# Holding back the first transfers, five dummy products fewer, and 2 MB of weights ahead of a store, in a two-layer mixture-of-experts trunk

## What is computed

```
for layer in (0, 1):
    if layer == 0:                       # mixer A: gated chunks; mixer B: sparse attention
        xn = rms_norm(x, mix_norm_even)
        proj = xn @ w_in                 # 512 x 1024 by 1024 x 2328
        au, av, q, kc, vc, ks, vs, kw, vw, gl = split(proj)
        x = x + concat(gating(au, av), attention(q, kc, ..., gl)) @ w_out
    else:                                # mixer C: windowed means of 2, 4, 8, 16 rows
        x = x + pool(rms_norm(x, mix_norm_odd))
    xn = rms_norm(x, ffn_norm[layer])
    # top 1 of 4 expert groups, then top 2 of its 8 experts, 32 experts in all
    x = x + sum over the chosen experts e of
            weight * ((silu(xn @ w_gate[e]) * (xn @ w_up[e])) @ w_down[e])
```

## Time and profile before

| | us |
|---|---|
| median of 3 executions | 809.83 (809.79 to 810.35) |
| the profiled execution, whole | 810.39 |
| its span, first to last instruction | 808.6 |
| TensorE busy in the span | 760.3 (94%) |
| VectorE busy | 259.3 (32%) |
| ScalarE busy | 251.2 (31%) |
| GpSimd busy | 104.0 (13%) |
| bytes moved | 258.69 MB, mean 320 GB/s |

### The profile page before, as it was taken

The page is one execution under the profiler, slowest core; times in us unless marked ns, Lnnn a source line. Parts: engine busy times, 40 slices in busy tenths (PEclk is TensorE's granted clock), DMA queues, the critical chain, the costliest instruction groups (busy, mean ns, idle before and its releaser), DMA issues.

```text
span 808.6 us, 9731 instructions
## 1 busy us (share of the span) xinstructions
PE 760.3 (94%) x3822; PEld 356.3 (44%) x3824; DVE 259.3 (32%) x654; ACT 251.2 (31%) x599; POOL 104.0 (13%) x170
## 2 busy tenths in 40 slices
PE   8999999999999999999988989979999999977987
PEld 7544544555555654333333333369333333332322
DVE  1011517675646365111110011376631111111015
ACT  4421346464444632121121112256222112111112
POOL 3000000000000001212422112250111121101111
PEclk9999999999999999999998989999999999999999
DMA  8995225132010679999999999999999999999998
GB/s 336 347 342 226 94 77 209 53 131 105 1 40 1 214 295 344 423 423 426 420 426 427 425 421 420 401 431 408 401 409 426 424 424 424 427 425 426 422 403 322
DMA packets 39703, 258.69 MB, mean 320 GB/s; under 512 B 8145, under 2 KB 8529, under 8 KB 26600
## 3 DMA queue, kind: packets, MB, share of 16 engines
q1 hardware_dynamic: 31016, 242.22, 74.0%
q0 software_dynamic: 8640, 15.83, 5.2%
HBM read 247.46 MB, written 26.21 MB: 338 GB/s over the span
## 4 chain that ended last, share of the span: by engine, by line
PE 85%; DMA 5%; DVE 4%; issue 4%; ACT 2%; SPq 0%; POOL 0%; POOLq 0%; DVEq 0%
PE ps L2202 28%; PE ps L2220 13%; PE ps L1893 12%; PE ps L2044 7%; PE ps L2196 4%; PE ps L1960 3%; PE ps L2102 3%; PE ps L1972 2%; PE ps L2111 2%; DMA norm<-expert_rows 2%; DMA expert_rows<-tmp 2%; PE ps L2149 2%; PE ps L1875 2%; PE ps L2209 1%; DVE x_rows L1308 1%
## 5 line engine op out<-in xcount | busy, mean ns | idle before, releaser
L2202 PE MATMUL ps<-w_pair,tmp 128*64 128x512 f32 x704 | 165.1, 620 | 17.3 <-issue 14.6
L2202 PEld LDWEIGHTS ps<-w_pair,tmp 128*64 128x64 f32 x704 | 52.8, 142 | 112.0 <-issue 105.9
L1893 PE MATMUL ps<-w_pair,norm 128*128 128x512 f32 (+1 forms) x256 | 98.6, 545 | 1.2 <-DMA w_pair<-in_w_in_chunk_dram 1.2
L1282 DVE TENSOR_TENSOR tmp<-tmp,ps 128x256 f32<-128x256 f32 x32 | 13.5, 421 | 249.0 <-ACT tmp L1141 249.0
L1141 ACT ACTIVATE tmp<-ps 128x256 f32<-128x256 f32 x32 | 12.3, 384 | 231.1 <-PE ps L2202 231.1
L2202 PE MATMUL ps<-norm,tmp 128*64 128x512 f32 x320 | 74.0, 617 | 6.0 <-issue 6.0
L2220 PE MATMUL ps<-w_pair,tmp 128*64 128x512 f32 x296 | 70.1, 599 | 1.1 <-ACT tmp L1144 0.9
L1893 PEld LDWEIGHTS ps<-w_pair,norm 128*128 128x128 f32 x256 | 48.2, 190 | 48.7 <-issue 44.4
L828 POOL DMA_INDIRECT expert_rows<-tmp x30 | 30.2, 1005 | 304.5 <-DVE tmp L1740 278.4
L822 POOL DMA_INDIRECT tmp<-norm_rows,tmp x30 | 31.1, 1035 | 262.1 <-DVE tmp L1660 237.7
L1740 DVE COPY tmp<-ps 128x512 f32<-128x512 f32 x30 | 20.8, 692 | 89.1 <-PE ps L2220 89.1
(11 more groups left out here) (288 smaller groups left out, 879.2 us busy)
## 6 DMA issues: line engine op xcount, KB each, us to landing
w_pair<-in_gate_up_by_row_dram SPq DMA_DIRECT2D x30, 2048.0 KB, 27.6
norm<-in_gate_up_by_row_dram SPq DMA_DIRECT2D x18, 2048.0 KB, 20.5
w_pair<-in_down_by_pair_dram SPq DMA_DIRECT2D x15, 2048.0 KB, 33.0
w_pair<-in_gate_up_by_row_dram SPq DMA_DIRECT2D x28, 1024.0 KB, 10.8
rest<-in_down_by_pair_dram SPq DMA_DIRECT2D x10, 2048.0 KB, 27.9
w_pair<-in_w_in_chunk_dram SPq DMA_DIRECT2D x4, 2048.0 KB, 14.6
norm<-expert_rows SPq DMA_DIRECT2D x16, 512.0 KB, 7.1
expert_rows<-tmp SPq DMA_DIRECT2D x1, 4096.0 KB, 41.6
```

The lines of the kernel that those rows point to most:

```text
L1282: return ve.tensor_tensor(out, in0, in1, op)
L1893: ins = mm(bank(4 + i % 4)[:, 0:n], xT[:, b, k, :], w[:, k, :], start=(k == 0), stop=(k == KD - 1))
L2202: ins = mm(o[64 * a:64 * a + 64, :], xT[:, k, 64 * a:64 * a + 64], gu[w][:, a, 2 * FE * k:2 * FE * (k + 1)], start=(k == 0), stop=(k == KD ...
```

## The change

Three places are edited. SyncE waits for block 0's columns and the gains (`s_gain`, 32) before it issues block 1's columns and everything behind them. Five of the ten dummy products with the identity are left out. In layer 1, expert 1's 2 MB of pair 2 are issued ahead of the store of block 3 and of the 0.5 MB of pair 4, instead of behind them.

```
             load_win(0, slice(0, 4))
             load_win(0, slice(4, KD))
+            sp.wait_ge(s_gain, 32)
             sp.dma_start(columns[1], t["x_by_column"][1]).then_inc(s_xc1, 16)
...
                     load_down_extra(1, back)
+                    load_gate_up(1, 2, 1)
                     store_rows(NB - 1)
                     load_down_early(1, 1)
-                    load_gate_up(1, 2, 1)
                     sp.wait_ge(s_st, 16 * NB * 2)
...
             pe_.wait_ge(s_const, 2)
-            for _ in range(10):
+            for _ in range(5):
                 mm(bank(7)[:, 0:P], ident[:, :], ident[:, :], start=True, stop=True)
```

## The result

| | before | after |
|---|---|---|
| median of 20 executions each, us | 809.89 (808.29 to 811.63) | 811.90 (810.56 to 813.60) |
| ratio, 95% interval | | 1.0024 (1.0018 to 1.0030) |
| profiled execution, whole / span, us | 810.39 / 808.6 | 810.56 / 808.8 |

The changed kernel is 2.0 us slower. The predicted 811.2 and its range hold the time, but the border of 811.4 for "slower by over 0.2%" is passed, and I had given that side 0.27. The profiled execution of the changed kernel is the fastest of its 20, so the two spans differ by 0.2 us only. A difference of two spans is therefore no measure here; the traces are read for what happens in them, and times are taken from medians and ratios.

What follows compares the result with a forecast made beforehand. The first chunk's transfer was taken to bound the start, the DMA engines layer 1. Terms 0 + 1.2 + 0.2 = 1.4 us more gave 811.2 median (811.8 profiled), range 807.9 to 812.8.

Steps and rivals of the forecast that it cites:

- Part 1: Start: SyncE's wait delays later issues 1.7 us, covered by chunk 0's transfer; cost 0, gain at most 2.6 us.
- Rival 1: Start: SyncE's issues disturb the chunk; held back, it lands at 6.2 to 7.5, giving 808.2; chance 0.28 with the filled hole.
- Part 2: Start: five dummies fewer widen TensorE's gap to 2.6 us and the clock falls; cost 1.2 us, bounds 0 and 1.4.
- 10 x 0.143 = 1.4 us: Start: ten of 20 dummy records, which take 2.86 us, are saved, so TensorE's dummies end at 6.0 instead of 7.43.
- on the far side of the gap that fell: Start: a 2.6 us gap lowers the clock, since it fell behind 1.93 us and not behind 1.41; a fall costs 1.7 us.
- what the first real product gains or loses goes through to the end of the first stage: First stage: the chain has no transfer behind the first product, so its shift of one or two us persists.
- Part 3: Layer 1, about 562 to 580 us: 2 MB ahead of the last store; 0.2 us lost, bounds 0 and 2.1.
- The queue is just long enough: Layer 1, store landing at 577.3: 0.5 MB, 1.2 us, still queued covers the restart, or runs dry for a moment.
- about a us: Layer 1, SyncE's release by the store: time a fresh issue needs to show in the transfer rate.
- Rival 3: Layer 1, 577 us: the DMA queue runs dry, 2.1 us; 813.1 with the clock's 1.2, 811.9 without; chance 0.10.
- the other hole (564 to 568): Layer 1: low rates of 315 and 209 GB/s; if the earlier 2 MB filled it, 1.6 us would come back.
- The gather: Layer 1: GpSimd's gather of pair 1's rows waits for the store; a us late delays TensorE under one, covered by later waits.

Runs made afterwards that it cites:

- hold: Only SyncE's wait for x's first columns and the gain added to the kernel before: 810.01 us against 810.17, ratio 1.0001.
- d5: Only five of the ten identity dummy products left out of the kernel before: 809.94 us against 810.17, ratio 1.0002.
- swap: Only layer 1's 2 MB of pair 2 moved ahead of the last store, against the kernel before: 811.06 us against 810.17, ratio 1.0014.
- hold_d5: The wait and five dummies fewer, without the 2 MB move, against the kernel before: 811.19 us against 809.95, ratio 1.0013 (0.9998 to 1.0028).
- after_fed: Whole change plus 1 MB of pair 4's down weights issued ahead of SyncE's store wait, against the kernel before: 810.30 us against 809.95, ratio 1.0009.
- d0: No identity dummy products, against the kernel before with ten: 811.35 us against 809.89, ratio 1.0020.
- d30: Thirty identity dummy products instead of ten, against the kernel before: 813.34 us against 809.89, ratio 1.0046.
- swap_fed: The 2 MB move plus 1 MB of pair 4's down weights ahead of SyncE's store wait, against the kernel before: 810.40 us against 809.89, ratio 1.0006.
- hold_swap: The wait and the 2 MB move, all ten dummies kept, against the kernel before: 811.89 us against 810.17, ratio 1.0022.
- swap_last: The 2 MB and also pair 4's 0.5 MB ahead of the store, against the kernel before: 812.47 us against 809.89, ratio 1.0029.

## Why the prediction was right and wrong

**Part 1, cost 0: right.** The second columns were issued at 4.41 (said: 4.3) and landed at 10.96, no later than before. TensorE's second block waited 0.34 us for their scaling in the changed kernel's trace, as they landed 3.0 us behind the chunk there, against 2.7 in the kernel before and in hold; in hold's trace the second block follows the first without such a wait, and hold alone is at +0.1 us. The reading of the slow rate as start-up and not as crowding holds as well: from 4 to 6 us the traces without the wait have 186 to 345 GB/s (d5 323, swap 327), those with it 228 to 327 (the changed kernel 244). The rate of these two us varies from execution to execution, and it is no sign of a crowd. Rival 1 falls with it: the chunk never landed ahead of 7.5.

**Part 2, cost 1.2: wrong for the changed kernel.** Two of its signs failed: the gap was 1.44 us and not 2.3 to 2.6, and no slow stretch came behind it. The first step that failed is "10 x 0.143 = 1.4 us", by which the dummies were to end at 6.0. The 20 records of the earlier trace rows do not have one pace, since the clock's first record in that trace is at 5.5 us, in the midst of them; five dummy products took 2.02 us in the changed kernel, 1.98 in hold_d5, 2.34 in after_fed and 1.43 in d5, where that record is at 4.9. Together with a chunk that landed at 7.98 instead of 8.56 this took 1.2 us off the gap. That d5 had a gap of 2.19 and hold_d5 one of 1.61 is the dummies alone: the chunk landed at 8.13 and 8.11.

The second is the rule that a gap is "on the far side of the gap that fell". The clock did fall behind the 2.19 us of d5, and the second block's products start at 13.74 there (the text said near 14). But a gap's length alone does not decide. In the trace that I had read, the clock stood at 1.00 behind a gap of 2.17 us at 527.96 and went to 0.50 behind those of 1.93 and 2.39 us; in the changed kernel's it stayed at 1.00 behind 2.38 us at 748.55 and went to 0.50 behind 1.54 us at 473.35. The Trainium skill (TensorE: Matmul & The Clock Gate, section Why this matters for your kernels) asks for no idle gap over about 3 us; these traces have the fall behind 1.54, 1.93, 2.19 and 2.39 us.

The third is "what the first real product gains or loses goes through to the end of the first stage", taken as the cost of the whole kernel. The shift of d5's trace is 1.5 us at layer 0's experts, 0.9 us in bytes at 760, and 0.2 us in the median of its executions, with 1.1 as the upper bound. d0 and d30, with larger shifts, arrive with 1.6 and 3.7. How much of a fall's 1.4 us would arrive stays open.

**Part 3, cost 0.2: wrong, and this was the result.** The orders came as described: the 2 MB landed at 574.9 (said: 576), the store at 576.1 (577.3), and SyncE issued the next load at 576.16. The step that failed is "Before, 2.5 MB or 6 us of transfers were queued at that moment; now only the 0.5 MB, 1.2 us ... The queue is just long enough". It has two faults. The first: it treats sixteen DMA engines as one that ends everything at one time. A transfer is spread over sixteen, and its landing is that of the slowest. By the semaphore events of the trace the sixteen ends of the store lie between 572.94 and 576.14 in the changed kernel, and between 570.18 and 572.44 before. Their ends of the 0.5 MB behind it begin at 574.1, and nine of sixteen had ended by 576.0: more than half of the engines had nothing left when SyncE was released at 576.1. So the rate falls from 574 on, 2 us ahead of the landing, which is what the windows show. The move does not make the spread: over the fourteen traces it lies between 2.3 and 3.9 us. The 6 us queued before cover it, 1.2 us don't. The Trainium skill (DMA: Bandwidth & Descriptors, section Why a DMA increments its semaphore by 16 and not by 1) says it: a transfer runs on up to sixteen engines which finish independently, and only the full count means that it has landed. The trace agrees, with 3.2 us between the first and the last. I knew the count and did not put it into the sum.

The second fault: the "about a us" until a fresh issue shows in the rate was taken as all that has to be covered. The windows of the changed kernel behind the issue at 576.16:

```profile
576.00:577.00 1.00, 1.00 (x4) 0.20 (x4) 0.93 (x3) 0.78 (x4) 0.01 (x1) 1.00 0.25 102
577.00:578.00 1.00, 1.00 (x8) 0.29 (x4) 0.90 (x6) 0.98 (x3) 1.00 (x1) 1.00 1.39 262
578.00:579.00 1.00, 1.00 (x8) 0.49 (x4) 0.90 (x7) 0.96 (x2) 0.06 (x1) 1.00 0.60 229
579.00:580.00 1.00, 1.00 (x7) 0.41 (x7) 1.00 (x3) 0.70 (x3) 0.00 (x0) 1.00 1.01 426
```

The full rate is back nearly 3 us behind the issue. My text had this slow start in its upper bound, from the rows at 154 us, and left it out of the 0.2. No run separates the two. An estimate from the changed kernel's trace: against the kernel before, some 1.0 MB or 2.4 us of the full rate are missing from 574 to 580; the store's sixteen ends are at 574.8 in the mean and SyncE is released at 576.1, so the spread has 1.3 us of it, and the restart the other 1.1.

Rival 3 had mechanism, place and price: 2.1 us and 811.9 without the clock, a window from 578 to 580 with a DMA share below 0.8 (it was 0.80, and 0.67 from 574 to 576). It came in at 1.6 us for the move alone and 811.90 for the whole. Its chance of 0.10 was too low for what its own price and rows said. The doubt about the other hole (564 to 568) told nothing: over all traces its rate goes from 262 to 418 GB/s, with and without the move.

**The gather: right.** It was released by the store and TensorE waited 0.63 us for it, and by swap_fed 1.71 us of such a wait went with +0.5 us at the end, while hold_swap had no such wait and +1.8.

**The sum.** 811.2 came from 1.2 in part 2 and 0.2 in part 3; by the runs of the parts it should have been about 0.2 and 1.6. That the time fell into the range, and near the forecast, is luck: two errors of opposite sign, with the loss forecast in another place than where it arose.

## What to carry to other kernels

Before you move a transfer ahead of one that is waited for, add up what is still queued behind the latter on each DMA engine, and ask that it covers the spread between the first and the last engine's end plus the restart until the full rate is back, not only the mean; when it doesn't, put an independent load between the store and the wait. Where a later stage runs at the full rate of the DMA engines, bytes that are not moved in a hole are the price of it, in us at that rate. What a delay of TensorE ahead of it costs is not known from its size: here a small one was lost in the noise and two larger ones arrived. And when two traces differ by less than the spread between executions, compare what is in them (bytes moved by a given time) and not their spans.

## What the runs showed of the hardware

- The sixteen DMA engines' ends of one transfer of 0.5 MB were 2.3 us apart before and 3.2 us in the changed kernel, and between 2.3 and 3.9 us over all fourteen traces.
- A queue of transfers that has run dry takes some us to be at the full rate again: in the changed kernel 426 GB/s were back at 579, nearly 3 us behind the issue at 576.16; in swap_last nothing moved from 578.0 to 578.5 behind the issue at 577.70, and the rate was 328 GB/s at 581.
- The start of the program has a spread of its own: the chunk's first half (0.6 MB) landed between 7.7 and 8.6 us, and 186 to 345 GB/s were moved from 4 to 6 us, whatever SyncE issued behind it.
- TensorE's clock went to its level of 1.2 GHz behind gaps of 1.54, 1.93, 2.19 and 2.39 us and stayed at 2.4 GHz behind gaps of 1.44, 2.17 and 2.38 us. One and the same wait, that ahead of pair 13 (2.4 us), was followed by 8.78 us for 32 records in the kernel before and by 7.09 in the changed kernel.
- In the thirteen traces with dummy products with the identity the clock's first record came between 4.7 and 7.8 us, so that ten dummy products took from 2.5 to 4.0 us. The windows give 1.00 ahead of that record too, where the pace of the products is slower.
